# Up and down products of an MLP as seven block products for eight, with row sums through memory

## The chip, the core and the metric

One core of one Trainium2 chip runs one inference step of a small hybrid decoder layer. The metric is the device time of that core in microseconds (us), median of several executions. TensorE multiplies matrices, VectorE (DVE), ScalarE (ACT) and GpSimd (POOL) work elementwise, SyncE (SP) issues the DMAs. The core has 8 PSUM banks, in which TensorE leaves its sums.

## What is computed

A layer works on 520 rows (512 of a prompt, 8 of a decode step) of width 2048, all in float32. The change touches its last third, the MLP, and the seams on both sides:

```python
D_FF = 4 * D_MODEL                       # 8192
...
x = x + concat(attention, ssd) @ w_out   # residual
h = rms_norm(x, ln_mlp)
u = square(relu(h @ w_up))               # (520, 8192)
x = x + u @ w_down                       # (520, 2048)
y = rms_norm(x, ln_final)
```

`w_up` and `w_down` hold 64 MB each and are read once.

## The kernel before

Activations lie transposed: 128 features on the partitions, 520 rows along them, in two halves of 260 (`HN`), which are one matmul's columns each. Full float32 precision is had by three matmuls per product: a weight block is split into a rounded part (`w_hi`) and the rest (`w_lo`), rows likewise, and w_hi x_hi + w_hi x_lo + w_lo x_hi are summed in PSUM.

Weights travel in pieces of 4 k-tiles x 256 columns (256 KB). `load_piece` (L634) issues a piece's two DMAs on SP's queue once its slot of four is free; `hi_piece` (L652) rounds it on ScalarE as soon as TensorE has used the piece two before; `lo_piece` (L661) subtracts on VectorE; `mul_piece` (L667, matmul at L677) issues 48 matmuls. Each engine runs its list in the order written, and semaphores that count pieces tie them together.

The MLP (`mlp_sp`, `mlp_pe`, `mlp_act`, `mlp_dve`, L2616 to L2733) runs over 8 chunks of 1024 of the 8192 columns. A chunk makes 4 up blocks (256 columns, 16 pieces in all), each followed by relu times the norm's factor (L2705), the square and the split of u (L2692, L2694, L2710), which stay in SBUF; and then 8 down blocks (16 pieces), each added to `x_acc` by `residual` (L2598). Before the first up product TensorE waits for the norm of the output projection's rows, whose squares GpSimd sums in `out_pool` (L2609), and GpSimd does the same for the final norm in `final_pool` (L2756). In the MLP GpSimd has nothing else to do.

## Time and profile before

| | |
|---|---|
| median of 3 runs | 2775.78 us (2770.29 to 2776.07) |
| span of the profiled execution | 2772.6 us |
| TensorE busy | 2641.4 us, 95%, 21237 matmuls |
| VectorE, ScalarE, GpSimd busy | 1136.5, 842.0, 105.0 us |
| MLP, first up to last down product | 1275.8 to 2752.3 us |
| granted TensorE clock, mean | 0.977 |

The page gives busy time and instructions of each engine, the chain of work that ended last, and groups of instructions with what ended the idle time before them. Matmuls are pipelined, so a matmul's own duration is longer than the distance from one to the next. Busy shares are means over the whole span; for one stage a stretch has to be read by itself.

### The profile page before, as it was taken

How to read it: one execution, taken by the hardware profiler on the slowest of the kernel's cores; microseconds unless marked ns; L12 is line 12 of the kernel's file. 1: busy time of each engine (PE TensorE's matmuls, PEld its weight loads, DVE VectorE, ACT ScalarE, POOL GpSimd, SP SyncE). 2: the span in 40 equal slices, each digit the busy share in tenths (PEclk: the TensorE clock that was granted, in tenths of full speed). 3: DMA queues.
4: the chain of work that ended last, by engine and by line, in shares of the span. 5: the costliest groups of instructions: out<-in, count | busy, mean ns of one | idle time of the engine just before them, and what ended most of it. 6: DMA issues, size and time to landing. Idle time of an engine off the chain costs nothing.

```text
span 2772.6 us, 50993 instructions
## 1 busy us (share of the span) xinstructions
PE 2641.4 (95%) x21237; PEld 2526.0 (91%) x21237; DVE 1136.5 (41%) x1712; ACT 842.0 (30%) x1360; POOL 105.0 (4%) x114
## 2 busy tenths in 40 slices
PE   7889999999799788999999999999999999999998
PEld 6779999998676557998999999999999999999998
DVE  4433224554886488333333323333333333333333
ACT  3242112223665355222212212222122122221233
POOL 0000000000000050110000000000000000000011
PEclk9999999999899888999999999999999999999999
DMA  5145333233004644222222222222222222222222
GB/s 215 61 164 159 93 95 93 74 96 107 3 31 129 206 130 130 92 92 78 90 93 95 87 95 91 90 91 91 91 91 91 91 91 91 91 91 91 91 91 92
DMA packets 241815, 274.64 MB, mean 99 GB/s; under 512 B 19397, under 2 KB 233811, under 8 KB 237494
## 3 DMA queue, kind: packets, MB, share of 16 engines
q1 hardware_dynamic: 238966, 237.88, 27.6%
q0 software_dynamic: 1728, 33.56, 3.2%
q10 hardware_dynamic: 1040, 2.10, 0.3%
q8 instruction: 54, 0.88, 0.1%
q14 instruction: 27, 0.22, 0.0%
HBM read 261.10 MB, written 20.71 MB: 102 GB/s over the span
## 4 chain that ended last, share of the span: by engine, by line
PE 86%; DVE 7%; ACT 3%; DMA 2%; issue 1%; POOL 0%; SPq 0%; ACTq 0%; DVEq 0%; POOLq 0%
PE PS L677 75%; PE PS L413 3%; ACT prob L1288 1%; PE PS L1240 1%; PE PS L1254 1%; PE PS L402 1%; DVE prob L1330 1%; DMA win_t<-kvs_tok 1%; DMA sel_t<-in_cache_kv_sel,idx_s 1%; DVE seg_ord L469 1%; PE PS L1482 1%; PE PS L365 0%; PE PS L1222 0%; DMA sel_x<-in_cache_kv_sel,idx_s 0%; DMA w<-in_cmp_w 0%
## 5 line engine op out<-in xcount | busy, mean ns | idle before, releaser
L664 DVE TENSOR_TENSOR w_lo<-w_raw,w_hi 128x1024 fp32r<-128x1024 f32 (+1 forms) x388 | 460.1, 1189 | 1322.0 <-ACT w_hi L658 1321.0
L658 ACT ACTIVATE w_hi<-w_raw 128x1024 fp32r<-128x1024 f32 (+1 forms) x388 | 395.6, 1024 | 1480.3 <-PE PS L677 1480.0
L677 PE MATMUL PS<-h_hi,w_hi 128*128 128x260 f32 x3360 | 675.5, 283 | 7.9 <-DVE h_lo L591 3.6
L677 PE MATMUL PS<-h_lo,w_hi 128*128 128x260 f32 x3360 | 675.2, 282 | 0.0
L677 PE MATMUL PS<-h_hi,w_lo 128*128 128x260 f32 x3360 | 673.9, 282 | 0.0
L677 PEld LDWEIGHTS PS<-h_hi,w_hi 128*128 128x128 f32 x3360 | 516.3, 189 | 9.3 <-DVE h_lo L591 3.7
L677 PEld LDWEIGHTS PS<-h_lo,w_hi 128*128 128x128 f32 x3360 | 519.2, 189 | 0.0
L677 PEld LDWEIGHTS PS<-h_hi,w_lo 128*128 128x128 f32 x3360 | 518.1, 189 | 0.0
L677 PE MATMUL PS<-u_hi,w_hi 128*128 128x260 f32 x2048 | 411.3, 282 | 8.4 <-DVE u_lo L2710 8.4
L677 PE MATMUL PS<-u_lo,w_hi 128*128 128x260 f32 x2048 | 410.5, 282 | 0.0
L677 PE MATMUL PS<-u_hi,w_lo 128*128 128x260 f32 x2048 | 410.0, 281 | 0.0
L677 PEld LDWEIGHTS PS<-u_hi,w_hi 128*128 128x128 f32 x2048 | 313.7, 188 | 10.1 <-issue 10.1
L677 PEld LDWEIGHTS PS<-u_lo,w_hi 128*128 128x128 f32 x2048 | 315.4, 188 | 0.0
L677 PEld LDWEIGHTS PS<-u_hi,w_lo 128*128 128x128 f32 x2048 | 314.7, 188 | 0.0
L677 PE MATMUL PS<-mix_hi,w_hi 128*128 128x260 f32 x512 | 103.6, 284 | 3.6 <-DVE w_lo L664 3.6
L677 PE MATMUL PS<-mix_lo,w_hi 128*128 128x260 f32 x512 | 103.5, 284 | 0.0
L677 PE MATMUL PS<-mix_hi,w_lo 128*128 128x260 f32 x512 | 103.2, 283 | 0.0
L2600 DVE TENSOR_TENSOR x_acc<-PS,x_acc 128x520 f32 (+1 forms) x144 | 93.3, 689 | 11.2 <-PE PS L677 11.2
L677 PEld LDWEIGHTS PS<-mix_hi,w_hi 128*128 128x128 f32 x512 | 79.3, 190 | 3.7 <-issue 3.7
L1288 ACT ACTIVATE prob<-PS,negmax 128x128 f32<-128x128 f32 (+3 forms) x128 | 65.8, 525 | 50.0 <-DVE negmax L1318 50.0
L677 PEld LDWEIGHTS PS<-mix_lo,w_hi 128*128 128x128 f32 x512 | 79.8, 191 | 0.0
L677 PEld LDWEIGHTS PS<-mix_hi,w_lo 128*128 128x128 f32 x512 | 79.5, 190 | 0.0
(455 smaller groups left out, 2304.5 us busy)
## 6 DMA issues: line engine op xcount, KB each, us to landing
w_raw<-in_w_up SPq DMA_DIRECT2D x256, 256.0 KB, 2.8
w_raw<-in_w_down SPq DMA_DIRECT2D x256, 256.0 KB, 2.9
w_raw<-in_w_in SPq DMA_DIRECT2D x160, 256.0 KB, 2.9
w_raw<-in_w_out SPq DMA_DIRECT2D x64, 256.0 KB, 3.1
out_kv_win_s<-in_state_kv_win SPq DMA_DIRECT2D x8, 1022.0 KB, 7.3
win_t<-in_state_kv_win SPq DMA_DIRECT2D x8, 896.0 KB
xtok<-in_x_prompt SPq DMA_DIRECT2D x4, 1024.0 KB, 8.0
st_s<-in_state_ssm SPq DMA_DIRECT2D x8, 512.0 KB, 5.0
```

The source lines that it names most:

```text
L402: last = e.transpose(PS[:, f % 4, x * P:x * P + P], seg_ord[:, c * NKV + g, j:j + 2, :].rearrange("p j d -> p (j d)"), ident[:])
L413: last = e.matmul(PS[:, 4 + 2 * c + r, :], w, x, start=(j + n == 0), stop=(j + n == 9))
L469: e.tensor_copy(seg_ord[:, c * NKV + g], seg_raw[:, :, c * NKV + g, :]).then_inc(c_order, 1)
L658: ins = e.activation(hi, raw, ACT.Copy)
L664: ins = e.tensor_tensor(lo, raw, hi.bitcast(F32), ALU.subtract)
L677: mm = e.matmul(PS[:, bank + 2 * m + h, 0:HN], w, x[:, k0 + k, h * HN:h * HN + HN], start=st and c == 0, stop=sp and c == 2)
L1240: last = e.transpose(PS[:, 4 + n, c0 + (qt - kt) * P:c0 + (qt - kt) * P + P], prob[:, u % 2, c:c + P], ident[:])
L1254: last = e.matmul(PS[x * HD:x * HD + HD, 7, kt * P:SEQ], kv_tok[:, kt, c:c + HD], probT(2 * s + x, kt), start=(b == 0 and kt == 0), stop=( ...
L1288: e.activation(prob[:, u % 2, P_OFF[qt]:P_OFF[qt] + w], PS[:, qt, 0:w], ACT.Exp, bias=negmax[:, u % 2, qt:qt + 1], accum_out=den[:, u % 2, ...
L1330: last = e.tensor_scalar(p, p, fac[:, u % 2, qt:qt + 1], None, ALU.mult)
L1482: last = e.transpose(PS[:, 4 + f % 3, y * P:y * P + P], src, ident[:])
L2600: e.tensor_tensor(x_acc[:, tile], PS[:, bank:bank + 2, 0:HN], x_acc[:, tile], ALU.add).then_inc(g_out, 1)
```

## The change

Up and down weights are seen as 2x2 blocks of 128x128 ("quads"), the 520 rows as two halves. The product of a 2x2 weight block with a 2x2 block of rows is formed from seven block products instead of eight, with sums of weight blocks and of row blocks as operands and sums of the seven results behind them.

- **Weights.** SP loads a quad (256x256, 256 KB) into `q_raw` (four slots). `quad_sums` on GpSimd makes three operations of 128, 256 and 128 elements, each behind the one before. `quad_hi` on ScalarE and `quad_lo` on VectorE split all seven operands (896 elements), four slots; the first waits until TensorE has used the quad four before. A load waits for the split of the quad four before.
- **Products.** `mul_quad` is 7 x 3 matmuls of 260 columns into seven banks, in order; at the first quad of a block it waits for each bank until the block before has been read (`up_free`, `down_free`). There are 32 up blocks of 8 quads and 48 down blocks of 4 or 6 quads (`CHUNKS`).
- **Rows of the up product.** `pair_raw`, `pair_sums`, `pair_hi`, `pair_lo` make seven operands for each of eight pairs of k-tiles; pairs 0 to 3 between output blocks, 4 to 7 behind the last. The norm's factor is made during up block 0.
- **Behind an up block.** `up_first` (ScalarE) and `up_read` (VectorE, five operations) bring the seven banks into `stage`, a single buffer, where relu, square and three row sums follow. SP stores it (`u_rows`, 932 KB a block) behind the load of quad 8p+5 of a later block, and both readers of a block wait until the store of the block before has landed.
- **Rows of the down product.** They are read back from memory, at quads listed by hand in `U_AT`, and split on ScalarE and VectorE (1820 elements).
- **Behind a down block.** `down_read` (VectorE) makes seven operations from the banks into `x_acc` and a sum `s_acc`.
- The final squares' sums on GpSimd move into its list of quads.

```diff
+CHUNKS = ((0, 4), (4, 4), (8, 6), (14, 6), (20, 6), (26, 6))
+PRODUCTS = ((0, 0), (6, 6), (4, 4), (2, 3), (5, 5), (1, 1), (3, 2))
...
+        stage = at("stage", [P, 8, HN], 4096)
...
+        u_rows = nc.dram_tensor("u_rows", (N_U, P, 7 * HN), F32, kind="Internal").ap()
...
+            e.wait_ge(w_used, OUT0 + 16)
+            for x in range(2):
+                e.wait_ge(w_hi_rdy, MLP0 - N_RAW + x + 1)
+                load_quad(e, x, w_u, x * PN, 0)
...
+        def pair_raw(e, j):
+            ln = lambda k: pcol[:, R_LNMLP + k:R_LNMLP + k + 1]
+            e.wait_ge(g_out, G_OUT0 + 2 * j + 2)
+            if j >= 2:
+                e.wait_ge(*h_T(4 * (j - 1)))
+            e.activation(x_raw7[j][:, 0, :], x_quad[:, j, 0, :], ACT.Copy, scale=ln(2 * j))
+            e.activation(x_b12[j % 2][:], x_quad[:, j, 1, :], ACT.Copy, scale=ln(2 * j))
+            e.activation(x_raw7[j][:, 1:3, :], x_quad[:, j, 2:4, :], ACT.Copy, scale=ln(2 * j + 1)).then_inc(h_raw.sem, 1)
+        def pair_sums(e, j):
+            r, b12 = x_raw7[j], x_b12[j % 2]
+            e.wait_ge(*h_raw(j + 1))
+            e.tensor_tensor(r[:, 6, :], b12[:], r[:, 2, :], ALU.subtract).then_inc(h_T.sem, 1)
+            e.tensor_tensor(r[:, 5, :], b12[:], r[:, 0, :], ALU.subtract).then_inc(h_T.sem, 1)
+            e.wait_ge(*h_T(4 * j + 1))
+            e.tensor_tensor(r[:, 4, :], r[:, 6, :], r[:, 0, :], ALU.subtract).then_inc(h_T.sem, 1)
+            e.wait_ge(*h_T(4 * j + 3))
+            e.tensor_tensor(r[:, 3, :], r[:, 1, :], r[:, 4, :], ALU.add).then_inc(h_T.sem, 1)
+        def pair_hi(e, j):
+            e.wait_ge(*h_T(4 * j + 4))
+            e.activation(x_hi7[j][:], x_raw7[j][:], ACT.Copy).then_inc(o_hi, 1)
+        def pair_lo(e, j):
+            e.wait_ge(o_hi, j + 1)
+            e.tensor_tensor(x_lo7[j][:], x_raw7[j][:], x_hi7[j][:].bitcast(F32), ALU.subtract).then_inc(o_lo, 1)
...
+            e.wait_ge(w_used, MLP0)
+            pair_raw(e, 4)
+            pair_raw(e, 5)
+            squares(e, OUT_BLOCKS - 1)
+            pair_hi(e, 4)
+            quad_hi(e, 2, 2)
+            pair_raw(e, 6)
+            pair_hi(e, 5)
+            quad_hi(e, 3, 3)
+            pair_raw(e, 7)
+            pair_hi(e, 6)
+            quad_hi(e, 4, 0)
+            pair_hi(e, 7)
...
+        def load_quad(e, s, w, row, col):
+            for x, places in enumerate((slice(0, 8, 7), slice(1, 3))):
+                e.dma_start(q_raw[s][:, places, :], w[bass.ds(row + x * P, P), bass.ds(col, PN)]
+                            .rearrange("p (a n) -> p a n", a=2)).then_inc(q_land[s].sem, 16)
+        def quad_sums(e, n, s, uses):
+            r = q_raw[s]
+            e.wait_ge(*q_land[s](32 * uses))
+            e.tensor_tensor(r[:, 6, :], r[:, 7, :], r[:, 0, :], ALU.subtract).then_inc(q_step, 1)
+            e.wait_ge(q_step, 2 * n + 1)
+            e.tensor_tensor(r[:, 4:6, :], r[:, 6:8, :], r[:, 2, :].unsqueeze(1).to_broadcast([P, 2, P]),
+                            ALU.add).then_inc(q_step, 1)
+            e.wait_ge(q_step, 2 * n + 2)
+            e.tensor_tensor(r[:, 3, :], r[:, 1, :], r[:, 4, :], ALU.subtract).then_inc(q_sum, 1)
+        def quad_hi(e, n, s):
+            e.wait_ge(q_sum, n + 1)
+            if not isinstance(n, int) or n >= N_Q:
+                e.wait_ge(*q_used(n - N_Q + 1))
+            e.activation(q_hi7[s][:], q_raw[s][:, 0:7, :], ACT.Copy).then_inc(q_hi.sem, 1)
+        def quad_lo(e, n, s):
+            e.wait_ge(*q_hi(n + 1))
+            e.tensor_tensor(q_lo7[s][:], q_raw[s][:, 0:7, :], q_hi7[s][:].bitcast(F32), ALU.subtract).then_inc(q_lo.sem, 1)
+        def mul_quad(e, n, s, x, first, last, free=()):
+            e.wait_ge(*q_lo(n + 1))
+            for bank, (wi, xi) in enumerate(PRODUCTS):
+                for at_bank, sem_, value in free:
+                    if at_bank == bank:
+                        e.wait_ge(sem_, value)
+                wh, wl, hi, lo = q_hi7[s][:, wi, :], q_lo7[s][:, wi, :], x_hi7[x][:, xi, :], x_lo7[x][:, xi, :]
+                for c, (w, v) in enumerate(((wh, hi), (wh, lo), (wl, hi))):
+                    mm = e.matmul(PS[:, bank, 0:HN], w, v, start=first and c == 0, stop=last and c == 2)
+                if last and bank < 5:
+                    mm.then_inc(b_done.sem, 1)
+            mm.then_inc(q_used.sem, 1)
+        def up_free(p):
+            if isinstance(p, int) and p == 0:
+                return ((0, g_out, G_MLP0 - 2), (4, g_out, G_MLP0))
+            return ((0, *b_first(p)), (1, *b_read(5 * p - 3)), (3, *b_read(5 * p - 2)), (4, *b_read(5 * p - 1)),
+                    (5, *b_read(5 * p)))
+        def down_free(b):
+            if isinstance(b, int) and b == 0:
+                return up_free(N_U)
+            r = 5 * N_U + 7 * b - 7
+            return ((0, *b_read(r + 2)), (1, *b_read(r + 3)), (2, *b_read(r + 4)), (3, *b_read(r + 5)),
+                    (4, *b_read(r + 6)), (5, *b_read(r + 7)))
...
+        def mlp_pe(e):
+            for j in range(N_X):
+                e.wait_ge(o_lo, j + 1)
+                mul_quad(e, j, j % N_Q, j, j == 0, j == N_X - 1, up_free(0) if j == 0 else ())
+                if j in (3, 5):
+                    rms_pe(e, j // 5)
+            with e.Fori(1, N_U) as p:
+                for j in range(N_X):
+                    mul_quad(e, p * N_X + j, j % N_Q, j, j == 0, j == N_X - 1, up_free(p) if j == 0 else ())
+            b0, n0 = 0, Q_UP
+            for q0, size in CHUNKS:
+                def block(b, n, s0):
+                    for j in range(size):
+                        e.wait_ge(*u_lo_rdy(q0 + j + 1))
+                        mul_quad(e, n + j, (s0 + j) % N_Q, (q0 + j) % 8, j == 0, j == size - 1,
+                                 down_free(b) if j == 0 else ())
+                step = 1 if size % N_Q == 0 else 2
+                if q0 == 0:
+                    block(0, n0, 0)
+                with e.Fori(1 if q0 == 0 else 0, N_X // step) as it:
+                    for m in range(step):
+                        block(it * step + (b0 + m), it * (step * size) + (n0 + m * size), m * size)
+                b0, n0 = b0 + N_X, n0 + N_X * size
...
+        U_AT = (248, 249, 251, 252, 257, 262, 267, 272, 289, 294, 299, 304, 316, 317, 325, 330,
+                362, 363, 364, 365, 373, 378, 410, 411, 412, 413, 421, 426, 458, 459, 460, 461)
+        def u_load(e, q):
+            e.wait_ge(*q_used(u_free_after(q) + 1))
+            e.wait_ge(u_kept, 16 * (q + 1))
+            if q >= 4:
+                e.wait_ge(*u_hi_rdy(q - 3))
+            e.dma_start(x_raw7[q % 8][:].rearrange("p k n -> p (k n)"), u_rows[q]).then_inc(u_ld[q % 4].sem, 16)
+        def u_high(e, q):
+            e.wait_ge(*u_ld[q % 4](16 * (q // 4 + 1)))
+            e.activation(x_hi7[q % 8][:], x_raw7[q % 8][:], ACT.Copy).then_inc(u_hi_rdy.sem, 1)
+        def u_low(e, q):
+            e.wait_ge(*u_hi_rdy(q + 1))
+            e.tensor_tensor(x_lo7[q % 8][:], x_raw7[q % 8][:], x_hi7[q % 8][:].bitcast(F32),
+                            ALU.subtract).then_inc(u_lo_rdy.sem, 1)
+        LD_LAG, HI_LAG, LO_LAG = 8, 6, 7
...
+        def u_store(e, p):
+            e.wait_ge(*u_T(3 * p + 3))
+            e.dma_start(u_rows[bass.ds(p, 1)].rearrange("a p n -> (a p) n"),
+                        stage[:, 0:7, :].rearrange("p k n -> p (k n)")).then_inc(u_kept, 16)
...
+            def up(p, z, first=False):
+                if not first:
+                    e.wait_ge(*q_lo(p * N_X + (z - N_Q + 1)))
+                load_quad(e, z % N_Q, w_u, z * PN, p * PN)
+            for z in range(2, N_X):
+                if z == 2:
+                    e.wait_ge(w_used, MLP0)
+                up(0, z, first=z < N_Q)
+            for z in range(N_X):
+                up(1, z)
+            with e.Fori(2, N_U) as p:
+                for z in range(N_X):
+                    up(p, z)
+                    if z == 5:
+                        u_store(e, p - 2)
+            for x, (q, m) in enumerate(QUADS):
+                n = Q_UP + x
+                e.wait_ge(*q_lo(n - N_Q + 1))
+                load_quad(e, n % N_Q, w_d, q * PN, m * PN)
+                if x in (5, 13):
+                    u_store(e, N_U - 2 + x // 13)
+                if n - LD_LAG in U_AT:
+                    u_load(e, U_AT.index(n - LD_LAG))
...
+        def mlp_pool(e):
+            quad_sums(e, 2, 2, 1)
+            quad_sums(e, 3, 3, 1)
+            with e.Fori(1, (Q_ALL - 48) // N_Q) as it:
+                for s in range(N_Q):
+                    quad_sums(e, it * N_Q + s, s, it + 1)
+            for n in range(Q_ALL - 48, Q_ALL):
+                quad_sums(e, n, n % N_Q, n // N_Q + 1)
+                if n - 4 in ENDED:
+                    final_pool(e, ENDED[n - 4] - 1)
+            final_pool(e, N_X - 2)
...
+        def up_first(e, p):
+            if not (isinstance(p, int) and p == 0):
+                e.wait_ge(u_kept, p * 16)
+            e.wait_ge(*b_done(p * 5 + 1))
+            e.activation(stage[:, 0, :], PS[:, 0, 0:HN], ACT.Copy).then_inc(b_first.sem, 1)
+        def up_read(e, p):
+            r = lambda n: p * 5 + n
+            if not (isinstance(p, int) and p == 0):
+                e.wait_ge(u_kept, p * 16)
+            e.wait_ge(*b_first(p + 1))
+            e.wait_ge(*b_done(r(3)))
+            e.tensor_tensor(stage[:, 7, :], stage[:, 0, :], PS[:, 2, 0:HN], ALU.subtract).then_inc(b_read.sem, 1)
+            e.wait_ge(*b_read(r(1)))
+            e.tensor_tensor(stage[:, 2, :], stage[:, 7, :], PS[:, 1, 0:HN], ALU.add).then_inc(b_read.sem, 1)
+            e.wait_ge(*b_read(r(2)))
+            e.wait_ge(*b_done(r(4)))
+            e.tensor_tensor(stage[:, 1, :], stage[:, 2, :], PS[:, 3, 0:HN], ALU.add).then_inc(b_read.sem, 1)
+            e.wait_ge(*b_done(r(5)))
+            e.wait_ge(*b_read(r(3)))
+            e.tensor_tensor(stage[:, 2:8:5, :], stage[:, 2:8:5, :],
+                            PS[:, 4, 0:HN].unsqueeze(1).to_broadcast([P, 2, HN]), ALU.add).then_inc(b_read.sem, 1)
+            e.wait_ge(*q_used(p * N_X + N_X))
+            e.wait_ge(*b_read(r(4)))
+            e.tensor_tensor(stage[:, 0:8:7, :], stage[:, 0:8:7, :], PS[:, 5:7, 0:HN], ALU.add).then_inc(b_read.sem, 1)
+        def up_relu(e, p):
+            e.wait_ge(*b_read(p * 5 + 5))
+            for h, rows_ in enumerate((slice(0, 2), slice(2, 8, 5))):
+                e.scalar_tensor_tensor(out=stage[:, rows_, :], in0=stage[:, rows_, :], scalar=0.0,
+                                       in1=rstd_bc[:, h].unsqueeze(1).to_broadcast([P, 2, HN]), op0=ALU.max,
+                                       op1=ALU.mult).then_inc(u_relu.sem, 1)
+        def up_square(e, p):
+            e.wait_ge(*u_relu(p * 2 + 2))
+            e.activation(stage[:, 0:3, :], stage[:, 0:3, :], ACT.Square).then_inc(u_sq.sem, 1)
+            e.activation(stage[:, 7, :], stage[:, 7, :], ACT.Square).then_inc(u_sq.sem, 1)
+        def up_sums(e, p):
+            e.wait_ge(*u_sq(p * 2 + 2))
+            e.tensor_tensor(stage[:, 6, :], stage[:, 7, :], stage[:, 2, :], ALU.subtract).then_inc(u_T.sem, 1)
+            e.wait_ge(*u_T(p * 3 + 1))
+            e.tensor_tensor(stage[:, 4:6, :], stage[:, 6:8, :],
+                            stage[:, 0, :].unsqueeze(1).to_broadcast([P, 2, HN]), ALU.subtract).then_inc(u_T.sem, 1)
+            e.wait_ge(*u_T(p * 3 + 2))
+            e.tensor_tensor(stage[:, 3, :], stage[:, 1, :], stage[:, 4, :], ALU.add).then_inc(u_T.sem, 1)
...
+            for n in range(5, N_X + 3):
+                quad_hi(e, n, n % N_Q)
+                if n in (7, 9):
+                    rms_act(e, n // 9)
+            up_first(e, 0)
+            def up(p, body=None):
+                for z in range(N_X):
+                    n = p * N_X + (z + 3)
+                    quad_hi(e, n, (z + 3) % N_Q)
+                    if z == 0:
+                        up_square(e, p - 1)
+                    if body:
+                        body(n)
+                up_first(e, p)
...
+        def down_read(e, b, first, last):
+            q0, size, m, n0 = BLOCKS[b]
+            r, d = 5 * N_U + 7 * b, 5 * N_U + 5 * b
+            x, s = x_quad[:, m], s_acc[m]
+            twice = lambda bank: PS[:, bank, 0:HN].unsqueeze(1).to_broadcast([P, 2, HN])
+            e.wait_ge(*b_done(d + 1))
+            if first:
+                e.tensor_copy(s[:], PS[:, 0, 0:HN]).then_inc(b_read.sem, 1)
+            else:
+                e.tensor_tensor(s[:], s[:], PS[:, 0, 0:HN], ALU.add).then_inc(b_read.sem, 1)
+            e.tensor_tensor(x[:, 0], x[:, 0], PS[:, 0, 0:HN], ALU.add).then_inc(b_read.sem, 1)
+            e.wait_ge(*b_done(d + 2))
+            e.tensor_tensor(x[:, 2:4], x[:, 2:4], twice(1), ALU.add).then_inc(b_read.sem, 1)
+            e.wait_ge(*b_done(d + 3))
+            e.wait_ge(*b_read(r + 1))
+            e.tensor_tensor(s[:], s[:], PS[:, 2, 0:HN], ALU.subtract).then_inc(b_read.sem, 1)
+            e.wait_ge(*b_done(d + 4))
+            e.wait_ge(*b_read(r + 3))
+            e.tensor_tensor(x[:, 2], x[:, 2], PS[:, 3, 0:HN], ALU.add).then_inc(b_read.sem, 1)
+            e.wait_ge(*b_done(d + 5))
+            e.tensor_tensor(x[:, 1:4:2], x[:, 1:4:2], twice(4), ALU.add).then_inc(b_read.sem, 1)
+            e.wait_ge(*q_used(n0 + size))
+            e.wait_ge(*b_read(r + 6))
+            e.tensor_tensor(x[:, 0:2], x[:, 0:2], PS[:, 5:7, 0:HN], ALU.add).then_inc(b_read.sem, 1)
+            if last:
+                e.wait_ge(*b_read(r + 7))
+                e.tensor_tensor(x[:, 1:4], x[:, 1:4], s[:].unsqueeze(1).to_broadcast([P, 3, HN]),
+                                ALU.add).then_inc(g_out, 2)
...
+            with e.Fori(1, N_U - 1) as p:
+                up(p)
+            up(N_U - 1, u_ops)
+            for b, (q0, size, m, n0) in enumerate(BLOCKS):
+                for n in range(n0 + 3, n0 + size + 3):
+                    if n < Q_ALL:
+                        quad_lo(e, n, n % N_Q)
+                        if n == Q_UP + 4:
+                            up_sums(e, N_U - 1)
+                        u_ops(n)
+                if b == 4:
+                    e.wait_ge(u_kept, 16 * N_U)
+                down_read(e, b, q0 == 0, q0 == CHUNKS[-1][0])
```

## Rows read from the trace of the kernel before

**Rows 1.** The page: an engine's busy time, and the chain that ended last.
```profile
PE 2641.4 (95%) x21237; PEld 2526.0 (91%) x21237; DVE 1136.5 (41%) x1712; ACT 842.0 (30%) x1360; POOL 105.0 (4%) x114
...
PE 86%; DVE 7%; ACT 3%; DMA 2%; issue 1%; POOL 0%; SPq 0%; ACTq 0%; DVEq 0%; POOLq 0%
```

**Rows 2.** Chain that ended last in order of time: start us, us, what.
```profile
1266.92 0.71 DVE x_acc L2600
...
1275.81 94.08 PE PS L677 x768
...
1554.07 1.07 ACT w_hi L658
...
1560.79 177.49 PE PS L677 x1488
1738.30 1.07 ACT w_hi L658
...
2752.28 0.71 DVE x_acc L2600
```

**Rows 3.** Timeline in an up block: start us, us, engine, line, operation.
```profile
1299.73 0.40 PE L677 MATMUL PS<-h_hi,w_hi 128*128 128x260 f32 x2
...
1305.42 0.40 PE L677 MATMUL PS<-h_hi,w_hi 128*128 128x260 f32 x2
```

**Rows 4.** Stretch inside the MLP: us, busy of PE, PEld, DVE, ACT, POOL, clock, DMA share, GB/s.
```profile
1500.00:2000.00 500.00, 496.84 (x4167) 496.23 (x4166) 161.52 (x175) 118.60 (x131) 0.00 (x0) 1.00 0.29 91
```

**Rows 5.** TensorE's clock around two idle gaps: timeline rows, and stretches (columns of rows 4).
```profile
194.22 0.80 PE L677 MATMUL PS<-h_hi,w_hi 128*128 128x260 f32 x2 [3.60 <-DVE h_lo L591]
...
1081.58 0.77 PE L677 MATMUL PS<-mix_hi,w_hi 128*128 128x260 f32 x2 [3.65 <-DVE w_lo L664]
...
194.00:198.00 4.00, 3.78 (x17) 3.78 (x18) 0.17 (x1) 3.71 (x4) 0.00 (x0) 0.50 0.64 197
198.00:202.00 4.00, 4.00 (x32) 4.00 (x31) 0.00 (x0) 0.00 (x0) 0.00 (x0) 0.88 0.35 105
...
1080.00:1085.00 5.00, 3.42 (x16) 3.45 (x17) 3.98 (x6) 4.97 (x8) 0.00 (x0) 0.50 0.43 135
1085.00:1090.00 5.00, 5.00 (x38) 5.00 (x38) 4.44 (x3) 0.29 (x2) 0.00 (x0) 0.85 0.22 75
...
1277.00:1280.00 3.00, 3.00 (x16) 3.00 (x15) 1.40 (x1) 0.00 (x0) 0.00 (x0) 0.50 0.00 0
```

**Rows 6.** Groups by form: count, busy us, mean ns, idle before and its releaser.
```profile
L664 DVE TENSOR_TENSOR w_lo<-w_raw,w_hi 128x1024 fp32r<-128x1024 f32 x356 | 439.4, 1235 | 1261.5 <-ACT w_hi L658 1260.5
L658 ACT ACTIVATE w_hi<-w_raw 128x1024 fp32r<-128x1024 f32 x356 | 377.2, 1060 | 1423.5 <-PE PS L677 1423.2
L2600 DVE TENSOR_TENSOR x_acc<-PS,x_acc 128x520 f32 x112 | 72.6, 689 | 0.0
L664 DVE TENSOR_TENSOR w_lo<-w_raw,w_hi 128x512 fp32r<-128x512 f32 x32 | 20.7, 687 | 60.5 <-ACT w_hi L658 60.5
L658 ACT ACTIVATE w_hi<-w_raw 128x512 fp32r<-128x512 f32 x32 | 18.4, 623 | 56.8 <-PE PS L677 56.8
```

**Rows 7.** GpSimd's two-input operations: min, median, max ns; and two in a row.
```profile
L2756 POOL TENSOR_TENSOR ssq_a<-ssq_a,sq x13: 1307/1312/1334, 2677.1 to 2746.0; 128x520 f32<-128x520 f32 x13
...
L1923 POOL TENSOR_TENSOR ce<-ebc,proj x16: 992/1004/1403, 995.7 to 1048.8; 128x384 f32<-128x384 f32 x16
...
2721.73 2.78 POOL L2756 TENSOR_TENSOR ssq_a<-ssq_a,sq 128x520 f32<-128x520 f32 x2 [8.65 <-ACT sq L2744]
```

**Rows 8.** Timeline of VectorE and of GpSimd where both read SBUF.
```profile
1271.04 2.06 DVE L664 TENSOR_TENSOR w_lo<-w_raw,w_hi 128x1024 fp32r<-128x1024 f32 x1 [0.16 <-ACT w_hi L658]
1268.99 3.03 POOL L2609 TENSOR_TENSOR ssq_a<-ssq_a,sq 128x520 f32<-128x520 f32 x2 [17.48 <-ACT sq L2558]
```

**Rows 9.** DMAs: landing of a 512 KB write and 1024 KB reads; SP issuing two.
```profile
L1880 SPq DMA_DIRECT2D out_ssm_p<-so x1: 372/372/372, 1062.8 to 1062.8; - x1
...
DMA to landing us min/median/max: 3.2/3.2/3.2
...
DMA to landing us min/median/max: 4.9/8.0/11.0
...
174.10 0.94 SPq L640 DMA_DIRECT2D w_raw<-in_w_in  x2
```

318 lines of the change are left out of this document (144 added, 174 removed).

## Prediction

> **What bounds the kernel now.** I began with the page's busy shares and the chain that ended last: TensorE is busy for 95% of the span, and line 677, the matmul of a weight piece, is 75% of the chain [rows 1]. The chain in order of time says where the MLP begins and ends: the last residual of the output projection starts at 1266.9, the first up product at 1275.8, the last down product ends at 2752.3; in between one chunk of eight follows another in 184.23 us (1554.07 to 1738.30) [rows 2]. The timeline gives the price of one matmul: 48 of them lie between 1299.73 and 1305.42, 118.5 ns each [rows 3]. A chunk has 1536 (8 up tiles x 16 k + 16 down tiles x 8 k, x 2 halves x 3 precision products), so 182.0 of its 184.23 us are matmuls one behind the other. VectorE and ScalarE are busy for 32% and 24% there, GpSimd not at all, the DMA engines for 29% [rows 4]. The MLP is bound by the number of its matmuls and by nothing else.
>
> **Products removed.** A quad (2x2 weight blocks of 128x128, seven block products with 260 columns, three matmuls each) is 21 matmuls where there were 24: 512 x 21 = 10752 for 12288. 1536 x 118.5 ns = **-182**. A quad is then 2.49 us of TensorE, an up block (8 quads) 19.9, a down block of six 14.9. The turnaround between up and down of a chunk also goes: 8 x 2.2 = **-18**.
>
> **The head.** Before, 9 us lie between residual and first up product, and after them TensorE runs at half clock for some microseconds [rows 2, 5]. After, the first four row pairs are ready early, but pairs 4 to 7 (three ScalarE copies, four VectorE sums, a split of 1820 elements on each engine) are made behind the last residual, with four weight splits between them: some 19 us of VectorE in a row while TensorE needs 12. I book **0** (-10 to +10).
>
> **One quad on the helpers.** Prices by size: ScalarE 1.060 us for 1024 and 0.623 for 512, so 0.95 for the 896 of a quad and 0.41 for 260; VectorE 1.235 and 0.687, so 1.10 for 896; with a PSUM operand 0.69 for 520, so 0.41 for 260 [rows 6]. GpSimd: 1.312 for 520 and 1.004 for 384, so 2.27 ns an element and 0.13 fixed: 0.42 + 0.71 + 0.42 for the three sums, plus 0.15 between dependent ones (2.78 for two of 1.31) = 2.0 us a quad alone [rows 7]. It isn't alone. Where GpSimd and a VectorE operation with both inputs in SBUF meet, one stands still: w_lo, begun at 1271.04, took 2.06 for 1.22 and ended 1.08 after GpSimd's 1272.02 (1268.99+3.03); x_acc, with one input in PSUM, stays at 0.689 [rows 6, 8]. So each split of a quad (0.93 of streaming) halts GpSimd, of which some 0.25 falls into its own gaps: **2.7 us a quad when GpSimd is busy throughout**, more than TensorE's 2.49. In the up product two relus and three sums of rows add 1.2 us a block (2.8 a quad), in the down product 32 splits of 1820 elements add 1.7 each (2.85 a quad).
>
> The Trainium skill (GPSIMD Engine Reference, Performance versus the Vector engine and Engine selection) advises against two-input elementwise work on GpSimd and times 2048 elements at 4497 ns. By that rate, an estimate, the 512 elements of a quad stream in 1.12 us for the 1.16 of the rows; six quads of the down product then take 16.9 for 17.1, and the whole 2899 for 2906.
>
> **The rows through memory: the wait that is added.** The buffer `stage` is single. `up_first(p)` and `up_read(p)` wait until the store of block p-1 has landed (`u_kept`), and SP issues this store only behind the load of quad 8(p+1)+5, which waits for the split of quad 8p+9, which waits for TensorE to have used quad 8p+5. Count from the start of the block's last quad (t=0): quad 8p+5 ends at -2.5, ScalarE's split at -1.4, VectorE's at -0.3, SP's two loads take 0.9 [rows 9], the store is issued at +0.7. A write of 512 KB lands after 3.2 us, a read of 1 MB after 4.9 at least [rows 9], so 932 KB take 4.6, and 0.3 behind the loads in the queue: landed at +5.6. Queued behind the wait are ScalarE's copy of bank 0 (0.41, to 6.0) and on VectorE the five reads (3 x 0.41 + 2 x 0.69 = 2.6, to 8.6), and behind these relus, splits and thereby SP's loads. TensorE wants bank 0 at +2.5 and gets it at 6.0; it wants bank 5 and gets it at 8.6, so the new block's first quad ends at 9.3 instead of 5.0: 4.35 us a block, 31 blocks, **+135** (2 to 6 us a block: 62 to 186). The store itself (twice 30 MB in all) is hidden otherwise, at 29% DMA share. While TensorE stands, GpSimd catches up (8 x 2.8 = 22.4 < 24.3), so the two costs don't add here.
>
> **The clock.** Each such stall leaves TensorE idle 3.5 us and halting for 3 more. Idle gaps of 3.65 and 3.60 us in this trace were each followed by a stretch at 0.50 of the clock, 1.2 for 2.4 GHz, with means of 0.50 and then 0.85 or 0.88 [rows 5]. In the 8.4 us from 1081.6 to 1090 there are 54 matmuls for 71 at 118.5 ns, in the 7.8 from 194.2 to 202 49 for 66: 2.0 us lost each time, taken for every block: **+62** (0 to 105; the whole of a half-clock stretch would cost 3.4).
>
> **The down product.** Seven accumulations per block (4 x 0.41 + 3 x 0.69 = 3.7 us) come behind the split of the quad two ahead, which ends at +2.2 of the last quad, while TensorE wants bank 0 again at +2.5 and gets it at 3.1, and bank 5 at about 5.9: 1.8 us a block. TensorE alone: 14.9 + 1.8 = 16.7 for six quads, 11.8 for four. GpSimd: 17.1 and 11.4. The larger each time: 32 x 17.1 + 16 x 11.8 = 736 for 637 of matmuls, **+99**. Rows read back in runs of four (1.7 on ScalarE and 2.0 on VectorE each, beside splits and reads) cost some 3 us five times: **+15**. In the last chunk 14 sums of squares of 1.46 us join GpSimd's queue: **+18**. The end: one read more, **+1**.
>
> **Sum.** -182 -18 +0 +135 +62 +99 +15 +18 +1 = +130. The profiled execution, 2772.6, becomes 2903; the median of the runs lies 3 above: **2906**.
>
> **Rivals.**
> (a) The clock holds through the stalls, as activity comes back in pieces: without its 62, 2844. For it: gaps of 1 us at the chunks cost none; against: both 3.6 us gaps did. 0.20.
> (b) The change as meant, and the one that ends faster: the store lands in time (it could only if issued about four quads earlier than my reading of the queues, or landed within 2 us), and splits fit into GpSimd's gaps. An up block is 19.9 + 0.7, down 723: -182 -18 +22 +86 +15 = -77, 2699. It decides from the point where the store has landed by +2 us. Against it: 3.2 us for half the bytes. 0.13.
> (c) The store lands in time but the engines do exclude each other: an up block is 22.4 for 26.3, 31 x 3.9 = 120 less, 2786. 0.08.
> (d) Exclusion costs little but the store is late: down 723 and sums of squares hidden, about 31 less, 2875. 0.10.
> (e) Small sums on GpSimd cost more than the line through 384 and 520 says (0.6 for 128): 3.5 us a quad, down 896 for 736, 3066. 0.07.
> (f) That the products aren't saved: the code issues 21 matmuls of unchanged shape a quad, so I give this nothing of its own.
> The forecast has 0.42. Measurement tells 0.2% (5.6 us) from no change. Faster: (b) and the lower end of (c), 0.16; within: 0.04; slower: 0.80. The range leaves out (b) and (e): 2780 to 2990.
>
> **What would show it.** After, the matmuls should number 10752 in the MLP at 118 ns in a run. Right if TensorE's gap at each up block's start is about 3.5 us, put down to `stage` or the DMA of `u_rows`; if POOL is busy around 70% in the down product with VectorE's split above 1.1 us; if half clock recurs every up block. Wrong if up blocks follow each other in under 22 us, if the store's landing is under 3 us, or if GpSimd's sums are not lengthened beside the splits.

## The result, and the profile after

| | before | after |
|---|---|---|
| median of the runs on one chip | 2775.9 us (2770.3 to 2781.2) | 2931.4 us (2929.1 to 2947.8) |
| span of the profiled execution | 2772.6 | 2927.4 |
| matmuls of the MLP | 12288 | 10752 |
| first up product to last down product | 1275.8 to 2752.3 | 1266.0 to 2904.0 |
| mean granted clock | 0.977 | 0.941 |

After to before is 1.0571, with an interval of 1.0539 to 1.0603: 1536 matmuls fewer, and 155 us more. (Ratios and intervals here are estimated over all runs; the medians' own quotient is 1.0560, and elsewhere too the two differ by up to 0.001.) The prediction was 2906 us, with a range of 2780 to 2990.

The page of the changed kernel; the first line answers to [rows 1], the others are the shares of the chain that ended last and the groups of the quads' own work (count | busy us, mean ns | idle before, its releaser):

```profile
PE 2594.0 (89%) x19701; PEld 2436.6 (83%) x19701; DVE 1715.9 (59%) x2432; ACT 1091.9 (37%) x1633; POOL 1319.0 (45%) x1650
...
POOL 30%; issue 15%; PE 15%; DVE 5%; POOLq 1%; DMA 1%; ACT 1%; SPq 0%; DVEq 0%; ACTq 0%
...
L2741 PE MATMUL PS<-x_hi,q_hi 128*128 128x260 f32 x3584 | 1075.8, 300 | 214.9 <-ACT stage L2876 109.6
...
L2729 DVE TENSOR_TENSOR q_lo<-q_raw,q_hi 128x896 fp32r<-128x896 f32 x512 | 628.9, 1233 | 451.0 <-ACT q_hi L2725 446.8
L2725 ACT ACTIVATE q_hi<-q_raw 128x896 fp32r<-128x896 f32 x512 | 485.3, 950 | 709.1 <-PE PS L2741 561.4
...
L2716 POOL TENSOR_TENSOR q_raw<-q_raw 128x256 f32<-128x256 f32 x512 | 494.8, 966 | 40.1
L2714 POOL TENSOR_TENSOR q_raw<-q_raw 128x128 f32<-128x128 f32 x512 | 304.6, 595 | 317.8 <-DMA q_raw<-in_w_up 206.4
L2719 POOL TENSOR_TENSOR q_raw<-q_raw 128x128 f32<-128x128 f32 x512 | 424.1, 828 | 40.1
```

Before, TensorE had 86% of the chain. Now it has 15% and GpSimd 30%, but these shares are no measure of what binds: this chain goes back only to 953.7 us (68% of the span), and in each up block it stays on GpSimd through 6 us in which GpSimd did nothing ("issue"). What binds has to be read at the seams, where one output block passes to the next. TensorE's busy time fell by only 47 us, though 182 us of matmuls are gone; a part of that is matmuls at half clock, of which the up product now has some 157 us. GpSimd's operations of 256 elements last 966 ns in the mean; their median, by line, is 739. Something lengthens a part of them.

**One seam between up blocks** shows nearly everything that the up product lost. Timeline (start us, us, engine, line, operation; in brackets the idle time before it and who ended it) of SP, ScalarE, TensorE and VectorE (TensorE's row is the new block's first matmul):

```profile
1560.21 0.35 SPq L2828 DMA_DIRECT2D u_rows<-stage  x1
...
1564.46 0.39 ACT L2876 ACTIVATE stage<-PS 128x260 f32<-128x260 f32 x1 [4.22 <-DMA u_rows<-stage]
...
1564.90 0.58 PE L2741 MATMUL PS<-x_hi,q_hi 128*128 128x260 f32 x1 [3.26 <-ACT stage L2876]
...
1564.98 0.42 DVE L2885 TENSOR_TENSOR stage<-stage,PS 128x260 f32<-128x260 f32 x1 [3.61 <-ACT stage L2876]
...
1567.27 0.70 DVE L2897 TENSOR_TENSOR stage<-stage,PS 128x520 f32<-128x520 f32 x1
```

and the stretches around it (us, busy of PE, PEld, DVE, ACT, POOL, then clock, DMA share, GB/s, as in [rows 4]):

```profile
1561.60:1564.90 3.30, 0.04 (x1) 0.00 (x0) 0.00 (x0) 0.42 (x2) 2.99 (x7) 0.80 0.92 305
1564.90:1569.60 4.70, 4.70 (x20) 4.40 (x21) 4.26 (x8) 1.17 (x2) 1.94 (x4) 0.50 0.00 0
1569.60:1575.00 5.40, 5.40 (x44) 5.40 (x44) 4.26 (x6) 2.71 (x4) 1.58 (x3) 0.93 0.33 97
```

The block's last quad begins at 1559.15. The store is issued 1.06 us later, lands after about 4.2, ScalarE's copy of bank 0 waited for it, and TensorE starts again at 5.75 with 3.26 us lost. Then it runs at 0.50 of its clock for 4.7 us, while VectorE reads the other banks. This seam is an early one: in the median of blocks 5 to 30 the store is issued at +1.20, lands 4.1 us later, and TensorE is back at +5.83. The time per block (from the first matmul of block 5 to that of block 30, divided by 25) is 25.76 us, of which eight quads back to back would be 19.9.

Where the waits of the whole execution stand (engine, line, waited for: us in total, times, longest):

```profile
ACT q_hi L2725 <- PE PS L2741: 561.4, 321, 8.2
ACT q_hi L2725 <- POOL q_raw L2719: 146.5, 75, 4.4
ACT stage L2876 <- DMA u_rows<-stage: 129.2, 31, 4.7
PE PS L2741 <- ACT stage L2876: 109.6, 32, 8.0
PE PS L2741 <- DVE x_acc L2965: 83.1, 47, 7.1
ACT x_hi L2815 <- DMA x_raw<-u_rows: 60.2, 30, 4.2
```

Each of three things has its row: the store (31 times), the down blocks' first bank (47 times), and the rows read back (30 times). ScalarE still waits more for TensorE than for GpSimd, so in this kernel GpSimd keeps up most of the time.

### The profile page after: what moved, and what is told of

Read it like the earlier page. It is cut to its first block, busy times and chain, and to the rows that moved or that the text cites. A ratio compares the mean times of both kernels' runs of the same rounds, so it can differ in the third digit from the quotient of the medians.

```text
span 2927.4 us, 53308 instructions
## 1 busy us (share of the span) xinstructions
PE 2594.0 (89%) x19701; PEld 2436.6 (83%) x19701; DVE 1715.9 (59%) x2432; ACT 1091.9 (37%) x1633; POOL 1319.0 (45%) x1650
## 4 chain that ended last, share of the span: by engine, by line
POOL 30%; issue 15%; PE 15%; DVE 5%; POOLq 1%; DMA 1%; ACT 1%; SPq 0%; DVEq 0%; ACTq 0%
POOL q_raw L2716 13%; POOL q_raw L2714 8%; POOL q_raw L2719 8%; PE PS L682 6%; PE PS L2741 6%; DVE q_lo L2729 1%; ACT q_hi L2725 1%; DMA x_raw<-u_rows 1%; POOLq L2715 1%; POOL ssq_f L3043 0%; DMA sel_t<-in_cache_kv_sel,idx_s 0%; POOLq L2718 0%; DVE x_lo L2819 0%; DVE x_acc L2978 0%; DVE x_acc L2967 0%
## 5 line engine op out<-in xcount | busy, mean ns | idle before, releaser
L2741 PE MATMUL PS<-x_hi,q_hi 128*128 128x260 f32 x3584 | 1075.8, 300 | 214.9 <-ACT stage L2876 109.6
L2741 PE MATMUL PS<-x_lo,q_hi 128*128 128x260 f32 x3584 | 1047.8, 292 | 0.0
L2741 PE MATMUL PS<-x_hi,q_lo 128*128 128x260 f32 x3584 | 1041.1, 290 | 0.0
L2741 PEld LDWEIGHTS PS<-x_hi,q_hi 128*128 128x128 f32 x3584 | 711.7, 199 | 262.3 <-ACT stage L2876 107.9
L2729 DVE TENSOR_TENSOR q_lo<-q_raw,q_hi 128x896 fp32r<-128x896 f32 x512 | 628.9, 1233 | 451.0 <-ACT q_hi L2725 446.8
L2725 ACT ACTIVATE q_hi<-q_raw 128x896 fp32r<-128x896 f32 x512 | 485.3, 950 | 709.1 <-PE PS L2741 561.4
L2741 PEld LDWEIGHTS PS<-x_lo,q_hi 128*128 128x128 f32 x3584 | 713.6, 199 | 0.0
L2741 PEld LDWEIGHTS PS<-x_hi,q_lo 128*128 128x128 f32 x3584 | 711.0, 198 | 0.0
L2716 POOL TENSOR_TENSOR q_raw<-q_raw 128x256 f32<-128x256 f32 x512 | 494.8, 966 | 40.1
L2714 POOL TENSOR_TENSOR q_raw<-q_raw 128x128 f32<-128x128 f32 x512 | 304.6, 595 | 317.8 <-DMA q_raw<-in_w_up 206.4
L2719 POOL TENSOR_TENSOR q_raw<-q_raw 128x128 f32<-128x128 f32 x512 | 424.1, 828 | 40.1
```

The lines of the kernel that those rows point to most:

```text
L2714: e.tensor_tensor(r[:, 6, :], r[:, 7, :], r[:, 0, :], ALU.subtract).then_inc(q_step, 1)
L2716: e.tensor_tensor(r[:, 4:6, :], r[:, 6:8, :], r[:, 2, :].unsqueeze(1).to_broadcast([P, 2, P]), ALU.add).then_inc(q_step, 1)
L2719: e.tensor_tensor(r[:, 3, :], r[:, 1, :], r[:, 4, :], ALU.subtract).then_inc(q_sum, 1)
L2725: e.activation(q_hi7[s][:], q_raw[s][:, 0:7, :], ACT.Copy).then_inc(q_hi.sem, 1)
L2729: e.tensor_tensor(q_lo7[s][:], q_raw[s][:, 0:7, :], q_hi7[s][:].bitcast(F32), ALU.subtract).then_inc(q_lo.sem, 1)
L2741: mm = e.matmul(PS[:, bank, 0:HN], w, v, start=first and c == 0, stop=last and c == 2)
```

## The experiments

All are the changed kernel with an edit; medians are compared with the kernel before on the same chip, which lay at 2775.2 to 2775.8. "Up block" is the mean from block 5 to block 30, "up" and "down" the whole products (after: 845.0 and 793.0 us).

### The store issued four quads earlier

```diff
-                    if z == 5:
+                    if z == 1:
                         u_store(e, p - 2)
...
-                if x in (5, 13):
-                    u_store(e, N_U - 2 + x // 13)
+                if x in (1, 9):
+                    u_store(e, N_U - 2 + x // 9)
```

> The store of a block's rows is issued behind the load of quad 8p+1 instead of 8p+5, four quads earlier; nothing else changes. If the late landing is what halts TensorE in the up product (my theory), the 3.4 us of idling per up block and the half clock behind it go, and an up block falls from 25.7 us to what GpSimd's sums beside VectorE's splits allow, 8 x 2.8 = 22.4: 31 x 3.3 = 102 us less, 2829. If GpSimd and VectorE don't hold each other up, it falls to 20.6 (matmuls and the reads): 158 less, 2773. If it is the order of the engines' lists (five reads behind a split) and not the landing, under 15 us are gained.

Measured: 2847.35 us, 1.0250 of before (1.0219 to 1.0281), 84 less than after. An up block takes 22.86 us, the up product 762.1; the down product stays at 791.7. The rows of waits on the banks' readers (L2887 is the second read):

```profile
PE PS L2741 <- ACT stage L2876: 30.4, 23, 11.9
...
PE PS L2741 <- DVE stage L2887: 29.6, 30, 1.1
```

ScalarE's copy no longer appears as waiting for the store. So the late store was worth 84 us, and only by its place in SP's list. The block does not fall to 19.9 plus its seam of 0.7, as it would if the store were all: some 2.3 us stay. Expected were 22.4 and 2829, if GpSimd sets the block then; and ScalarE's waits for GpSimd do rise from 146.5 to 362.9 us.

### GpSimd's weight sums over 8 of 128 columns

The three sums keep their count and waits but cover 8 columns (from quad 4 on). The remaining columns are left out.

```diff
-            e.tensor_tensor(r[:, 6, :], r[:, 7, :], r[:, 0, :], ALU.subtract).then_inc(q_step, 1)
+            e.tensor_tensor(r[:, 6, 0:8], r[:, 7, 0:8], r[:, 0, 0:8], ALU.subtract).then_inc(q_step, 1)
```

> GpSimd's three sums of a quad are made over 8 of 128 columns (from quad 4 on; the rest of the sums is left out), with all waits kept: its time per quad falls from 2.0 us to well under 1, and it leaves VectorE's splits alone. By my theory the up blocks stay at 25.7 us, as the store's landing sets them, and only the down product gains, where I put the exclusion at 13 and the sums of squares at 18 of the sum: from 793 to 740-760, 2880-2900. If GpSimd is the limit of the whole MLP, the up blocks fall to 22 or below as well and the whole to 2800 or less. If the exclusion costs nothing, 2931.

Measured: 2890.63 us, 1.0412 (1.0388 to 1.0435), 41 less than after. Up blocks stay as they were, 25.6 us; the first one, of the head, takes 33.0 for 38.6. The down product takes 762.9 for 793.0, its last chunk 133.0 for 142.9. The changed kernel's up product hides GpSimd beneath the store's wait, as the prediction had it ("the two costs don't add here"); the down product doesn't. Its blocks of six without row splits stay at 16.57 us with narrow sums too, except in the last chunk, where they go from 18.38 to 16.57: only there is it GpSimd, with the final squares' sums in its list, that binds such blocks.

### Filler matmuls in the stall

Thirteen matmuls of constants into the free eighth bank ahead of each up block from the second on, so that TensorE isn't idle while it waits.

```diff
             with e.Fori(1, N_U) as p:
+                for _ in range(13):
+                    e.matmul(PS[:, 7, 0:P], ones[:], ident[:], start=True, stop=True)
                 for j in range(N_X):
```

> Thirteen 128x128 float32 matmuls of constants into the unused bank 7 (about 2.8 us) are put ahead of each up block from the second on, where TensorE stands idle for 3.1 to 3.4 us. They change nothing but TensorE's activity. If the fall to half clock costs the 2 us a block that I booked, the up block goes from 25.7 to 23.7 us and the whole to 2869. If the restart is bound by the five reads of the banks and the half clock hides beneath them, the time stays within 10 us of 2931.

Measured: 2917.77 us, 1.0510 (1.0489 to 1.0531), only 13.6 less than after. The filler did what it should; a seam's timeline and stretches (columns as above; the 13 matmuls stand as 26 records):

```profile
1556.09 3.06 PE L2770 MATMUL PS<-ident,ones 128*128 128x128 f32 x26
1559.38 0.39 ACT L2879 ACTIVATE stage<-PS 128x260 f32<-128x260 f32 x1 [4.14 <-DMA u_rows<-stage]
1559.82 0.39 PE L2741 MATMUL PS<-x_hi,q_hi 128*128 128x260 f32 x1 [0.66 <-ACT stage L2879]
...
1560.84 0.39 PE L2741 MATMUL PS<-x_hi,q_hi 128*128 128x260 f32 x1 [0.39 <-DVE stage L2890]
...
1560.00:1564.50 4.50, 3.97 (x28) 3.35 (x28) 4.14 (x8) 0.97 (x2) 1.78 (x4) 1.00 0.00 0
```

The clock stays at 1.00 where after had 0.50 and then 0.93. Half-clock stretches wholly inside the up product number 2 instead of 31, 14 us instead of 157. But a block still takes 25.15 us. The first quad falls from 4.71 to 3.94 and the second from 2.70 to 2.50, and that is all, for TensorE now waits for each bank's read (0.39 for line 2890's) where it used to be too slow to have to; 0.36 goes back: from the last quad's start to the new block's first matmul it is 6.24 us for 5.88, as the store is now issued at +1.63 (median) for +1.20. Half the clock was mostly hidden beneath VectorE's five reads. This is the step of my prediction that failed by size: 62 us booked, 14 measured (15 in the up product).

### The down banks read before the last split

```diff
                 for n in range(n0 + 3, n0 + size + 3):
+                    if n == n0 + size + 2:
+                        ...
+                        down_read(e, b, q0 == 0, q0 == CHUNKS[-1][0])
                     if n < Q_ALL:
                         quad_lo(e, n, n % N_Q)
...
-                down_read(e, b, q0 == 0, q0 == CHUNKS[-1][0])
```

> In the down product VectorE makes a block's seven reads of the banks before the split of the quad two ahead instead of behind it. If the reads' start is what halts TensorE for 1.8 us at each of 48 block seams, and GpSimd keeps up with TensorE once it is rid of them, 86 us go: 2845. By my forecast GpSimd's 2.7 to 2.85 us a quad stands right behind: a block of six goes from 16.6 only to about 16.2, and the whole gains 15 to 30 us: 2900 to 2915. If the seams are bound by something else, nothing changes.

Measured: 2897.93 us, 1.0442 (1.0417 to 1.0468), 33.5 less than after; the down product takes 763.3. Blocks of six in which no rows are split take 14.96 us, six quads back to back, where after had 16.53 to 16.74: the seam of 1.6 to 1.8 us is gone. The last chunk doesn't gain (145.2 for 142.9), and blocks with row splits take 18 to 21. Those aren't bound by the seam.

### All three places in the lists at once

The early store, the down swap, and the same swap at the up blocks: `up_first` before the last `quad_hi` of the block, `up_read` before the last `quad_lo`.

```diff
                 for z in range(N_X):
                     n = p * N_X + (z + 3)
+                    if z == N_X - 1:
+                        up_first(e, p)
                     quad_hi(e, n, (z + 3) % N_Q)
...
-                up_first(e, p)
```

> Three changes of order together: the store four quads earlier, the down blocks' reads before the split of the quad two ahead, and the same for the up blocks (ScalarE's copy of bank 0 before its split, VectorE's five reads before its split). The first two alone gave 84 and 33 us. If GpSimd's sums beside VectorE's splits set the up block at 22.4 to 22.9 us, the order of the up reads gives nothing more: 2810 to 2820. If the reads set it, the block falls to 20.1 us: 2730.

Measured: 2793.55 us, 1.0070 (1.0047 to 1.0093), 138 less than after. An up block takes 22.01 us: 2.75 a quad, with seams and store out of the way. This lies between the two expectations (2810 to 2820, 2730): the reads' place did cost something in an up block (22.86 falls to 22.01), but what stands behind it is well above 20.1. A stretch of the up product of after, and the same stretch here, with this kernel's waits of ScalarE:

```profile
1500.00:1900.00 400.00, 348.18 (x2610) 340.36 (x2610) 230.57 (x276) 140.73 (x171) 280.37 (x379) 0.90 0.38 120
```

```profile
1500.00:1900.00 400.00, 378.34 (x3057) 366.84 (x3057) 302.37 (x325) 162.20 (x200) 370.19 (x437) 1.00 0.45 139
...
ACT q_hi L2725 <- POOL q_raw L2719: 618.8, 344, 5.0
ACT x_hi L2815 <- DMA x_raw<-u_rows: 91.6, 32, 9.9
```

GpSimd is busy for 92.5% of the stretch and the clock is whole. ScalarE waits 344 times for GpSimd, where it was 75. By the next run this is the bound that the store had covered.

### The same with narrow weight sums

```diff
-            e.tensor_tensor(r[:, 3, :], r[:, 1, :], r[:, 4, :], ALU.subtract).then_inc(q_sum, 1)
+            e.tensor_tensor(r[:, 3, 0:8], r[:, 1, 0:8], r[:, 4, 0:8], ALU.subtract).then_inc(q_sum, 1)
```

> The kernel with all three changes of order, and GpSimd's sums over 8 of 128 columns (from quad 4 on, the rest of the sums left out). With the store and the reads out of the way my theory leaves GpSimd as the limit: the up block falls from 22.9 to about 20.1 us (87 us less), and the down product from some 763 to 700; together 2670. The sums of weight blocks on GpSimd would then cost 150 us. If something else stands there (VectorE's own load, the rows read back), under 40 us go.

Measured: 2677.7 us, 0.9653 (0.9625 to 0.9682), 116 less than with all three places changed. The same columns of the weight sums are left out as in the first narrow run.

```profile
1500.00:1900.00 400.00, 400.00 (x3360) 400.00 (x3359) 275.01 (x361) 176.87 (x220) 168.52 (x480) 1.00 0.49 151
```

TensorE isn't idle in 400 us; 3360 matmuls there are 119.0 ns each. An up block takes 20.01 us. Here the seven products for eight show in the time, 98 us under the kernel before, and GpSimd's sums alone cost 116. Even here something stands in front in the down product: it takes 720.4 us for 637 of matmuls, and its slow blocks of six (16 to 20 us for 15) lie where rows are read back. The narrow sums take away GpSimd's own time and its meetings with VectorE together, and no run separates the two. But where VectorE reads PSUM banks, as in the seam shown first, GpSimd goes from one quad's sums to the next's in some 1.9 us (1563.39 to 1565.32), under TensorE's 2.49; so by that estimate it is the meetings that put it above.

### The third weight sum on VectorE

Of the three sums, the last (`r[:, 3] = r[:, 1] - r[:, 4]`) goes to VectorE, one quad ahead of the split.

```diff
+        def quad_three(e, n, s):
+            r = q_raw[s]
             e.wait_ge(q_step, 2 * n + 2)
             e.tensor_tensor(r[:, 3, :], r[:, 1, :], r[:, 4, :], ALU.subtract).then_inc(q_sum, 1)
...
             e.tensor_tensor(q_lo7[s][:], q_raw[s][:, 0:7, :], q_hi7[s][:].bitcast(F32), ALU.subtract).then_inc(q_lo.sem, 1)
+                quad_three(e, n + 1, (s + 1) % N_Q)
```

> As the kernel with all three changes of order, and the third sum of each quad (128 elements) on VectorE, behind the split of the quad before; GpSimd keeps two. GpSimd then needs 1.4 us a quad alone and 2.1 beside a split, VectorE 1.5 and with reads, relus and row splits 2.2 to 2.4, both under TensorE's 2.49. If GpSimd's own serial chain is the limit, the up block falls from 22.9 to about 20.7 us and the down product by 25: 2725. If it is the time for which both engines together hold the shared way to SBUF, that is the same as before, and under 20 us go. If VectorE becomes the bound, it is slower than with GpSimd's third sum.

Measured: 2929.06 us, 1.0559 (1.0532 to 1.0586): 135 us slower than the same kernel with all sums on GpSimd. A miss, and by its waits and its timeline a chain:

```profile
ACT q_hi L2730 <- DVE q_raw L2724: 915.2, 450, 5.6
...
2400.66 1.09 DVE L2734 TENSOR_TENSOR q_lo<-q_raw,q_hi 128x896 fp32r<-128x896 f32 x1 [1.02 <-ACT q_hi L2730]
2401.67 0.28 DVE L2724 TENSOR_TENSOR q_raw<-q_raw 128x128 f32<-128x128 f32 x1
2401.98 0.95 ACT L2730 ACTIVATE q_hi<-q_raw 128x896 fp32r<-128x896 f32 x1 [1.36 <-DVE q_raw L2724]
...
2402.97 1.63 DVE L2734 TENSOR_TENSOR q_lo<-q_raw,q_hi 128x896 fp32r<-128x896 f32 x1 [1.02 <-ACT q_hi L2730]
```

VectorE makes the sum of a quad (0.28), then waits for ScalarE's rounding of the same quad (0.95 behind it), then splits (1.09 or 1.63): 2.3 to 2.9 us a quad in series, with GpSimd idle for half the time. GpSimd was relieved, and the round trip between VectorE and ScalarE became the bound.

### The rows split later

To the kernel with all three places changed, the read, the rounding and the split of the rows read back now lie 8, 7 and 8 quads behind their place in the list, for 8, 6 and 7.

```diff
-        LD_LAG, HI_LAG, LO_LAG = 8, 6, 7
+        LD_LAG, HI_LAG, LO_LAG = 8, 7, 8
```

> As the kernel with all three changes of order, and the splits of the rows read back from memory one quad later in ScalarE's and VectorE's lists. In the changed kernel's trace ScalarE stands 4 us before such a split for the read to land, with the weights' splits queued behind it, and the last block of each of the chunks takes 22 us for 16.6. If that wait is what costs there, 2.5 us of it go at each of the ten or so places: 15 to 25 us less than with the three changes alone. If the rows' own lateness costs TensorE, nothing is gained, or a few us are lost.

Measured: 2764.35 us, 0.9966 (0.9953 to 0.9978), 29 less than with the old lags.

```profile
ACT x_hi L2815 <- DMA x_raw<-u_rows: 33.0, 25, 3.9
```

ScalarE's wait for the rows falls from 91.6 to 33.0 us, the down product from 770.6 to 748.8. So ScalarE stood in line for rows that weren't there yet, and the weights' rounding behind it. Of the 28 us between the two profiled executions 22 lie in the down product and 2 in the up product; the other 4 lie ahead of the first up product, where the edit changes nothing, and that start lies anywhere between 1261.0 and 1271.3 in the profiled executions of the changed kernel and its edits.

### The third sum on VectorE, two quads ahead

```diff
-                quad_three(e, n + 1, (s + 1) % N_Q)
+                quad_three(e, n + 2, (s + 2) % N_Q)
```

> As the kernel with all changes of order and the row splits one quad later (2764), and the third sum of each quad on VectorE, but made two quads ahead of its split and not one, so that ScalarE's split never waits for a sum queued behind VectorE's split of the quad before. With one quad ahead this cost 135 us. If that was the chain through three engines (0.43 + 0.95 + 1.2 = 2.6 us a quad and longer at the seams), it goes, and GpSimd's shorter chain shows: up blocks of 20.7 for 22.0 us, 2720. If it was the time for which VectorE and GpSimd hold the way to SBUF, or VectorE's load, the time stays above 2850.

Measured: 2841.6 us, 1.0245 (1.0227 to 1.0262), with the later lags underneath. Neither expectation (2720; above 2850) was met. That is 87 less than one quad ahead (of which up to 29 are the lags), and 77 more than with all sums on GpSimd.

```profile
DVE q_raw L2725 <- POOL q_raw L2719: 321.3, 271, 4.7
...
ACT q_hi L2731 <- DVE q_raw L2725: 449.3, 253, 5.6
```

Much of the round trip is gone, but now VectorE itself waits in line for GpSimd, 321 us in all, and the split and the bank reads stand behind that wait. Which part of the 77 is that, and which the load standing behind a later split, these runs don't tell apart.

### The final sums of squares on VectorE

With the later lags, `final_pool` moves from GpSimd's list to VectorE's.

```diff
-                if n - 4 in ENDED:
-                    final_pool(e, ENDED[n - 4] - 1)
-            final_pool(e, N_X - 2)
...
                         u_ops(n)
+                    if n - 2 in ENDED:
+                        final_pool(e, ENDED[n - 2] - 1)
```

> As the kernel with all changes of order and the row splits one quad later (2764), and the 14 sums of squares of the final norm on VectorE (0.7 us each) instead of behind GpSimd's quads (1.3 us each). In the last chunk six blocks take 18.6 us for 15.0 to 16 in the other chunks; if that is GpSimd's queue, they fall to about 16.5, 12 us less: 2752. If the final norm's own chain or ScalarE's part sets them, nothing changes.

Measured: 2754.22 us, 0.9932 (0.9914 to 0.9950). The last chunk takes 141.2 us for 149.0, its blocks of six 16.8 to 17.7 for 18.6. One sum of 520 elements costs VectorE 0.775 us (median; on GpSimd 1.317). This version leaves nothing out and is 0.7% faster than the kernel before, 177 us faster than the change as it was made.

## Why the prediction was right

Sign and size came out: +155 us in the profiled execution where the sum had +130. The time was in part luck, as two steps missed in opposite directions. By its steps:

| step | booked | measured | from |
|---|---|---|---|
| products | -182 | -182 | 10752 matmuls; 20.01 us an up block with narrow sums |
| turnarounds of a chunk | -18 | -20 | before: 1476.5 us less 12288 at 118.5 ns |
| head | 0 (-10 to +10) | +12 | first two up blocks 67.9 us for 46.2, started 9.8 us earlier |
| an up block's seam | 6.35 us: 4.35 store, 2.0 clock | 5.8: 5.2 and 0.6 | filler run |
| down product over its matmuls | +132 | +156 | 793.0 less 637 |
| last up block, beyond the others | 0 | +5 | 30.6 for 25.8, with the first rows read back in it |
| GpSimd when busy throughout | 22.4 an up block (2.8 a quad) | 22.0 | three places changed |
| end | +1 | +3 | 23.4 us behind the last product, for 20.3 |

The up product with its head ends at 2111.0; the sum had it at about 2110. The down product holds nearly all of the difference. Three terms do not follow from their own parts, none of them enough to change the forecast: 8 x 2.7 + 1.2 gives 22.8 an up block, not 22.4; 32 splits of 1.7 us over 256 quads give 2.9 a quad in the down product, not 2.85; and 14 sums of 1.46 us are 20, not 18.

**The store: right, in place and in size.** In the seam shown it was issued at +1.06 (said: +0.7), landed about 4.2 us after its issue (said: 4.9, of it 0.3 behind the loads), and TensorE was back at +5.75 (said: 6.0). The issue was 0.4 us later and the landing 0.7 quicker than said, so that the quarter of a microsecond flatters; but which load stands ahead of the store, and which split ahead of that load, had been read rightly, and moving the store in the list gave 84 us back.

**The clock: the step that failed.** That half clock would follow each stall was right, 31 times. Its price was not. I took it from gaps behind which TensorE had nothing to wait for [rows 5]. Here the engine that ran slower was itself behind VectorE's five reads, which take 3.0 us from the copy of bank 0 on; at full clock it only waits more. The filler run measured 0.6 us a block for 2.0. The store step in turn was 0.9 us short (4.35 booked, 5.2 left when the clock is whole): in the filler run TensorE comes back at +6.24 instead of +6.0, the reads end 3.06 us after that instead of 2.6, and the last two products come 0.9 behind them instead of 0.7. The two errors partly cancel (1.4 too much, 0.9 too little), and the seam of 5.8 for 6.35 looks better than its parts were: that is luck. In the down product the clock was at half too, in some 14 stretches, 67 us together, where the kernel before had none and the sum booked nothing; what they cost there no run shows.

**The head: a little outside its bounds.** The up product begins 9.8 us earlier than before, but its first two blocks take 67.9 us for the 46.2 that the sum gives them. The first gap in TensorE's timeline:

```profile
1278.53 0.56 PE L2741 MATMUL PS<-x_hi,q_hi 128*128 128x260 f32 x1 [7.13 <-DVE q_lo L2729]
```

and three more of 1.0 to 2.6 us, all put down to VectorE's split, follow. The split of quad 2 was late because ScalarE's rounding was, and that waited for GpSimd:

```profile
1269.75 2.84 POOL L2698 TENSOR_TENSOR ssq_a<-ssq_a,sq 128x520 f32<-128x520 f32 x2 [15.43 <-ACT sq L2606]
...
1273.28 2.41 POOL L2716 TENSOR_TENSOR q_raw<-q_raw 128x256 f32<-128x256 f32 x1
...
1276.25 0.95 ACT L2725 ACTIVATE q_hi<-q_raw 128x896 fp32r<-128x896 f32 x1 [4.44 <-POOL q_raw L2719]
```

The last squares' sums stood ahead of quad 2 in GpSimd's list, and one of its operations then took 2.41 us for 0.74 while VectorE made row sums and splits. I had counted VectorE's row of work alone and left GpSimd out of the head. With narrow sums (quads 2 and 3 keep full ones) the first gap stays at 7.1 us and the first block is 5.5 us shorter, but it begins 3.6 us later, so that it ends only 1.9 us earlier; how much of the head's 12 us the sums of the later quads cost stays open.

**GpSimd beside VectorE: right.** The same operation of GpSimd, free and beside a split:

```profile
2562.31 0.74 POOL L2716 TENSOR_TENSOR q_raw<-q_raw 128x256 f32<-128x256 f32 x1
...
2563.96 1.08 DVE L2729 TENSOR_TENSOR q_lo<-q_raw,q_hi 128x896 fp32r<-128x896 f32 x1
2564.13 1.52 POOL L2716 TENSOR_TENSOR q_raw<-q_raw 128x256 f32<-128x256 f32 x1
```

0.74 becomes 1.52 where a split of 1.08 us was under way, while VectorE's reads with one input in PSUM keep their 0.69 and cost nobody anything. Over the whole execution, GpSimd's operations of 256 elements that meet no VectorE operation with both inputs in SBUF take 0.72 to 0.75 us (164 of 512, 84 of them beside a read of a PSUM bank); the others go up to 2.43. The Trainium skill (SBUF — State Buffer, SBUF: two separate sides) says that VectorE and GpSimd share a pair of ports that one instruction holds until it ends, and that two SBUF inputs on VectorE are enough to want it against a GpSimd operation that reads SBUF; the rows agree: the sum ends about 0.6 us after the split does, as if it had stood for all of it. Priced from rows of other operations [rows 7, 8], a quad came to 2.7 us and 2.8 in an up block, and the kernel whose other waits were gone showed 2.75 there. By its narrow-sum twin this is 116 us.

**The down product: right as a mechanism, uneven in size.** The seam was 1.6 to 1.8 us (six quads in 16.53 to 16.74; said: 16.7), shown by its removal: 14.96. But GpSimd was not what bound the quiet blocks (said: 17.1), as they keep their 16.57 with narrow sums. It was busy for 81% of the down product, where the prediction's sign was around 70%. A down seam (start, us; the last two of its PE rows begin the next block):

```profile
2564.09 0.39 PE L2741 MATMUL PS<-x_hi,q_hi 128*128 128x260 f32 x1 [0.17 <-DVE x_acc L2978]
...
2578.15 0.39 PE L2741 MATMUL PS<-x_hi,q_hi 128*128 128x260 f32 x1 [0.62 <-DVE x_acc L2965]
...
2580.83 0.39 PE L2741 MATMUL PS<-x_hi,q_hi 128*128 128x260 f32 x1 [0.17 <-DVE x_acc L2978]
```

From 2564.09 to 2580.83, bank 5 to bank 5 of the next block, is 16.74 us. In such a block sums and split keep step with the quads: of GpSimd's three operations from 2567.97 on only the last meets the split (0.46, 0.74, 1.20), and the next quad's first begins at 2570.48: 2.51 us a quad, not 2.7. The step that failed in this term is the price of the rows read back: 15 booked. Three six-quad chunks took 144.5 to 146.3 us for 139.8 by the sum, and the two four-quad chunks 108.7 and 105.8 for some 97. The last took 142.9 for 155: the final squares' sums, booked at 18 beside GpSimd's 17.1 a block, cost it some 10 (133.0 with narrow sums). One place of rows read back, at the end of a chunk (a block of 22 to 23 us instead of 16.6):

```profile
2500.35 1.73 ACT L2815 ACTIVATE x_hi<-x_raw 128x1820 fp32r<-128x1820 f32 x1 [4.11 <-DMA x_raw<-u_rows]
2501.98 2.62 ACT L2725 ACTIVATE q_hi<-q_raw 128x896 fp32r<-128x896 f32 x3
2502.95 1.26 DVE L2729 TENSOR_TENSOR q_lo<-q_raw,q_hi 128x896 fp32r<-128x896 f32 x1 [5.59 <-ACT q_hi L2725]
```

ScalarE stands 4.11 us before a rounding whose rows hadn't landed, and everything of the weights behind it. I had priced the 1.7 us of work of these operations but not the wait ahead of them, though it is the same kind as the store's, which I had counted through. Putting the operations one quad later gave 29 us (22 of them in the down product).

**The rivals.** "The clock holds" (2844) is out as a mechanism, as the clock fell, though the filler run shows that a held clock would have given 2918, not 2844. "The store lands in time but the engines exclude each other" was given 2786; made on purpose by the early store it is 2847, by all three places 2794. Of the 61 us between the first two, 25 are the sum's own miss; 31 are an up block that fell from 25.76 to 22.86 where 26.3 to 22.4 was booked. "As meant" was given 2699; only with the three places changed and the sums narrowed, a kernel that leaves out most of the sums, is it 2678. "Exclusion costs little but the store is late" was given 2875; with narrow sums and the late store it is 2891. "Small sums cost 0.6 us" is out: alone they take 0.46.

## What to carry to other kernels

Fewer products on the bounding engine are worth their time only if each helper's list still runs ahead of it: write down, for one block, when each operation is issued, what stands before it in the list, and what it waits for. Here 1536 matmuls fewer were worth 182 us (by count, at 118.5 ns); five places in the helpers' lists cost 177, which came back by moving lines with no work removed (the last of the five from GpSimd's list to VectorE's), and the added weight sums another 116. A stall hides other costs under it (GpSimd's bound, half the clock), so take it away alone before you price what lies beneath; and moving a sum from a busy engine to one that a third engine waits for can make a chain longer than the work it relieves.

## What the runs showed of the hardware that I had not expected

- Half clock behind a stall cost 0.6 us a block, not the 2 to 3 us that its length suggests, where the banks were being read at the same time.
- GpSimd's two-input sums alone take 0.46 us for 128 elements and 0.74 for 256 (medians 462 to 466 and 739 ns over all), close to the line drawn through 384 and 520. Over 8 and 16 elements they took 0.20 and 0.22 alone, and 0.29 to 0.39 in the mean, as some still stood beside a VectorE split for up to 2 us.
- VectorE isn't always the winner of a collision: its split of 896 elements lasts 1.08 us when it begins first and 1.63 when GpSimd's sum does, in the rows shown (medians in the changed kernel behind 1300 us: 1.09, and 1.25 for the 341 splits that began during a sum).
- A store of 932 KB lands after 4.1 us (4.0 to 5.1), and after 4.5 (4.4 to 5.5) when it is issued four quads earlier. Reading the same rows back takes 5.5 (4.9 to 8.0).
